# Streamed expert weights: quarters moved one seat ahead, gates stored by token tile, and transposes reordered

## What is computed

```
merged = g_pool * y_pool + g_attn * y_attn
x = x + merged @ w_out[l]
h2 = rmsnorm(x, ffn_norm_g[l])
...
for e in range(N_EXPERTS):
    g = jnp.minimum(t @ w_gate[e] + b_gate[e], SWIGLU_LIMIT)
    u = jnp.clip(t @ w_up[e] + b_up[e], -SWIGLU_LIMIT, SWIGLU_LIMIT)
    act = (u + 1.0) * (g * jax.nn.sigmoid(SWIGLU_ALPHA * g))
    out = out + comb[:, e:e + 1] * (act @ w_down[e] + b_down[e])
```

## Time and profile before

| | |
|---|---|
| median of three runs | 1081.67 us |
| profiled execution | 1081.04 us |
| its span in the trace | 1079.2 us |
| TensorE busy | 1040.2 us (96%) |
| DVE, ACT, POOL busy | 274.8, 198.6, 29.5 us |
| read from HBM | 432.14 MB |
| granted TensorE clock | 0.999 of full speed |

### The profile page before, as it was taken

How to read it: one execution, slowest core, us unless ns; L and a number is a source line. 1 busy time by engine, 2 the same in 40 slices (tenths; PEclk the granted TensorE clock), 3 DMA queues, 4 the chain that set the end, 5 groups by cost and what they waited for, 6 DMA issues and landing times.

```text
span 1079.2 us, 12157 instructions
## 1 busy us (share of the span) xinstructions
PE 1040.2 (96%) x5114; PEld 445.0 (41%) x5114; DVE 274.8 (25%) x560; ACT 198.6 (18%) x347; POOL 29.5 (3%) x41
## 2 busy tenths in 40 slices
PE   9999999999999999999999999999999999999997
PEld 5889984333333333333333333333333333333332
DVE  6876753111111111111111111111111111111121
ACT  4657532111110111111111111111111001110111
POOL 0070020000000000000000000000000000000000
PEclk9999999999999999999999999999999999999999
DMA  9835999999999999999999999999999999999996
GB/s 316 302 104 179 387 390 383 394 428 427 434 431 428 438 428 431 427 437 432 430 430 431 436 430 432 428 437 431 431 430 432 435 430 432 422 428 429 427 425 275
DMA packets 37235, 433.75 MB, mean 402 GB/s; under 512 B 5030, under 2 KB 7627, under 8 KB 19659
## 3 DMA queue, kind: packets, MB, share of 16 engines
q1 hardware_dynamic: 36704, 432.64, 95.7%
q10 hardware_dynamic: 490, 0.56, 0.1%
HBM read 432.14 MB, written 1.05 MB: 401 GB/s over the span
## 4 chain that ended last, share of the span: by engine, by line
PE 76%; DMA 12%; ACT 6%; DVE 4%; issue 1%; SPq 0%; DVEq 0%
PE ps L1027 55%; DMA ring<-in_exp_w_up 11%; PE ps L932 5%; PE ps L979 5%; ACT arena L1336 3%; PE ps L679 2%; PE ps L681 2%; PE ps L680 2%; PE ps L1035 2%; DVE ring_r L1522 2%; PE ps L973 1%; DMA ring<-in_w_in 1%; ACT ring_r L1198 1%; ACT arena L1371 1%; PE ps L941 0%
## 5 line engine op out<-in xcount | busy, mean ns | idle before, releaser
L1027 PE MATMUL ps<-ring,arena 128*64 128x512 f32 x2432 | 538.4, 595 | 15.0 <-ACT arena L1371 11.3
L1027 PEld LDWEIGHTS ps<-ring,arena 128*64 128x64 f32 x2432 | 168.0, 137 | 339.0 <-issue 316.3
L1027 PE MATMUL ps<-arena 128*64 128x512 f32 x640 | 142.0, 595 | 5.0 <-ACT arena L1371 3.1
L1773 DVE TENSOR_TENSOR arena<-ps,gain 128x512 f32<-128x512 f32 x32 | 22.1, 692 | 275.6 <-PE ps L973 275.6
L1798 DVE TENSOR_SCALAR arena<-ps 128x512 f32<-128x512 f32 x30 | 20.8, 692 | 261.8 <-PE ps L1027 261.8
L1027 PEld LDWEIGHTS ps<-arena 128*64 128x64 f32 x640 | 44.4, 137 | 89.1 <-issue 85.2
L1336 ACT COPY arena<-ps 128x512 f32<-128x512 f32 x32 | 33.8, 1055 | 249.7 <-PE ps L932 249.7
L1375 ACT COPY arena<-ps 128x256 f32<-128x256 f32 x30 | 11.2, 372 | 293.3 <-PE ps L979 293.3
L1811 DVE TENSOR_SCALAR arena<-ps 128x512 f32<-128x512 f32 x31 | 21.4, 692 | 170.9 <-PE ps L1027 170.9
L979 PE MATMUL ps<-arena 64*128 64x512 f32 x256 | 63.9, 616 | 0.0
L932 PE MATMUL ps<-arena 128*64 128x512 f32 x256 | 60.6, 593 | 0.0
(11 more groups left out here) (231 smaller groups left out, 658.7 us busy)
## 6 DMA issues: line engine op xcount, KB each, us to landing
ring<-in_exp_w_up SPq DMA_DIRECT2D x19, 4096.0 KB, 29.3
ring<-in_exp_w_down SPq DMA_DIRECT2D x18, 4096.0 KB, 28.4
ring<-in_exp_w_gate SPq DMA_DIRECT2D x18, 4096.0 KB, 29.8
ring<-in_exp_w_down SPq DMA_DIRECT2D x12, 2048.0 KB, 39.1
ring<-in_exp_w_up SPq DMA_DIRECT2D x11, 2048.0 KB, 40.4
ring<-in_exp_w_gate SPq DMA_DIRECT2D x10, 2048.0 KB, 40.7
arena<-in_exp_w_gate SPq DMA_DIRECT2D x5, 4096.0 KB, 29.8
arena<-in_exp_w_down SPq DMA_DIRECT2D x5, 4096.0 KB, 30.4
```

What stands on the lines that cost most here:

```text
L1027: last = mm(ps[BLOCK * to:BLOCK * (to + 1), bank, :], src[:, c, half, :], moved, start=(fresh and half == 0 and c == 0), stop=(half == 1 a ...
L1773: v.tensor_tensor(h_in, ps[:, 6, :].rearrange("p (c h s) -> p c h s", c=4, h=2), wide(gain[:].rearrange("p h c -> p c h"), [P, 4, 2, BLOCK ...
```

## The change

It does five things.

1. **Gates by token tile.** The 16 gate blocks, the merged rows and their high and low parts are stored tile by tile (`tile_pair`, `both_tiles`, `m_split`), through access patterns of 2 x 128 columns instead of 256. No instruction is added.
2. **Early rows.** After part (0,1) of the output projection, tile 0's halves of `early_place` and `late_place` are free. SP sends 0.5 MB to each there, and the other 0.5 MB to each after the last part.
3. **Matrices moved up by a quarter.** For n = 6 to 14 the first quarter of matrix n goes to a free seat of the hold before it (`moved_up`). Before, seat 1 of hold 0 stayed empty from the end of the first half of matrix 0 until matrix 10. For n = 11 to 14 the first quarter is sent after the first half of matrix n-5, and 3 MB after the second.
4. **The rolled loop waits one half later.** Matrix 14 has its first quarter in hold 3, and so on, so matrix 15 must wait until matrix 11 has let go of its quarter in hold 0. The rule is in the loop's code and thus holds for n = 15 to 74: each is issued after the first half of matrix n-4, no longer at the end of matrix n-5.
5. **Halves only for the last pair** (`FINE = E - 2`): the nine matrices of experts 27 to 29 come as 4 MB. And **transposes in another order** (`turns`): gather, `turn_weights`, `turn(7)`, `turn(6)`, down product.

```diff
-        FINE = E - 5
+        FINE = E - 2
@@
         def halved(n, rolled=False):
-            return not rolled and (HOLDS <= n < PASS or n >= MATRICES * FINE)
+            return not rolled and (HOLDS <= n <= 2 * HOLDS or n >= MATRICES * FINE)
+
+        def moved_up(n, q):
+            if (n, q) == (HOLDS, 0):
+                return early_place
+            if n % HOLDS == 0 and q:
+                k, p = 0, (0, 1, 3)[q - 1]
+            elif q:
+                k, p = n % HOLDS, q - 1
+            else:
+                k, p = (n - 1) % HOLDS, 2 if n % HOLDS == 1 else 3
+            return hold(k)[:, p // 2, 2 * D * (p % 2):2 * D * (p % 2 + 1)]
@@ load_matrix
-                if n >= HOLDS or not isinstance(base, int):
+                if not isinstance(base, int):
+                    sp.wait_ge(piece_done, of_round + both_halves + 1)
+                elif n >= HOLDS:
                     sp.wait_ge(piece_done, of_round + (first_half if halves else both_halves))
@@ load_first_holds
+                sp.wait_ge(wo_done, wo_count(0, 1))
+                sp.dma_start(late_place[:, 0:D], flat_rows(0)[:, 6 * D:7 * D]).then_inc(early_rows_in, 16)
+                sp.dma_start(early_place[:, 0:D], first_down[:, 0, 0:D]).then_inc(early_rows_in, 16)
@@
+                sp.wait_ge(piece_done, 2 * HOLDS)
+                sp.dma_start(moved_up(2 * HOLDS, 0), quarter_of(2 * HOLDS, 0)).then_inc(wrapped_in, 16)
+                sp.wait_ge(piece_done, 2 * HOLDS + 2)
+                sp.dma_start(hold_front[:, 0:4 * D], flat_rows(2 * HOLDS)[:, 2 * D:6 * D]).then_inc(matrix_in[0], 16)
+                sp.dma_start(moved_up(2 * HOLDS, 3), quarter_of(2 * HOLDS, 3)).then_inc(lower_in[0], 16)
+                for n in range(2 * HOLDS + 1, PASS):
+                    k = n % HOLDS
+                    sp.wait_ge(piece_done, 2 * (n - HOLDS) + 1)
+                    sp.dma_start(moved_up(n, 0), quarter_of(n, 0)).then_inc(quarter_in[k][0], 16)
+                    sp.wait_ge(piece_done, 2 * (n - HOLDS) + 2)
+                    sp.dma_start(hold(k).rearrange("p h x -> p (h x)")[:, 0:6 * D],
+                                 flat_rows(n)[:, 2 * D:]).then_inc(matrix_in[k], 16)
@@ tensor
+            def turns(i):
+                pe.wait_ge(pick_ready, i + 2)
+                gather()
+                pe.wait_ge(expert_step, 2 * i + 2)
+                turn_weights(5)
+                pe.wait_ge(act_ready, i + 1)
+                turn(7, act_out).then_inc(act_T, 1)
+                pe.wait_ge(hg_ready, i + 2)
+                turn(6, h_got).then_inc(h_turned, 1)
@@ expert
-                pe.wait_ge(pick_ready, i + 2)
-                gather()
-                pe.wait_ge(act_ready, i + 1)
-                turn(7, act_out).then_inc(act_T, 1)
-                turn_weights(5)
+                turns(i)
                 pe.wait_ge(actT_ready, i + 1)
                 product(r, step, MATRICES * j + 2, 7, actT, fresh=True)
-                pe.wait_ge(hg_ready, i + 2)
-                turn(6, h_got).then_inc(h_turned, 1)
```

More of the change, by code:

```diff
@@ L173, in build, with tile_pair, both_tiles @@
         y_split = pair(places["u"], places["p"], NG)
-        m_split = pair(places["gate"], places["gate"] + NC * S, NC)
+        tiles = gate.rearrange("p c s -> p (c s)").rearrange("p (b t c s) -> p b t c s", b=2, t=NT, c=NC)
+        m_split = tuple(rounded(places["gate"] + NC * S * b, NC * S).rearrange("p (t c s) -> p t c s", t=NT, c=NC)
+                        for b in range(2))
+        def tile_pair(m):
+            return tiles[:, m // NC, :, m % NC, :]
+        def both_tiles(ap):
+            return ap.rearrange("p (t s) -> p t s", t=NT)
         h_normed = gate[:, 0:NC, :]
@@ L889, in project @@
                         columns_of = both(split_slot(WO_P), ALL, m)
-                    last = mm3(wo_sum(t, half, part), both(m_split, ALL, m, slice(P * t, P * (t + 1))), columns_of,
+                    last = mm3(wo_sum(t, half, part), both(m_split, ALL, t, m), columns_of,
                                start=(m == 0), stop=(m == NC - 1))
@@ L993, in product @@
                 first_pass = isinstance(r, int) and isinstance(step, int)
+                moved_on = first_pass and HOLDS <= n < 3 * HOLDS
                 by_quarters = first_pass and HOLDS <= n < 2 * HOLDS
@@ L1003, in product @@
                                     pe.wait_ge(landed, r * 16 + 16)
-                        if by_quarters and c == 0:
-                            pe.wait_ge(quarter_in[at][half], 16)
+                        if c == 0 and (by_quarters or moved_on and half == 0):
+                            pe.wait_ge(*((wrapped_in, 16) if n == 2 * HOLDS else (quarter_in[at][half], 16 * (n // HOLDS))))
                         if n == HOLDS - 1 and first_pass and half == 0 and c == 0:
@@ L1008, in product @@
                         if n == 0 and first_pass and half == 1 and c == 2:
+                            pe.wait_ge(early_rows_in, 32)
                             pe.wait_ge(last_quarter_in, 16)
-                        if n not in TAIL and c == (2 if by_quarters else 0):
+                        if n not in TAIL and c == (2 if moved_on else 0):
                             if half == 0:
@@ L1019, in product @@
                             row = late_place[:, D * (c - 2):D * (c - 1)]
-                        elif n == HOLDS and first_pass and half == 0:
-                            row = early_place[:, D * c:D * (c + 1)] if c < 2 else hold_chunks(at)[:, 0, c - 2, :]
+                        elif moved_on:
+                            row = moved_up(n, 2 * half + c // 2)[:, D * (c % 2):D * (c % 2 + 1)]
                         for to in range(2):
@@ L1247, in gate_tanh @@
                 strip_wait(act, s)
-                strip_release(fn(gate[:, c, :], strip_bank(s)[:, 0:S], ACT.Tanh, bias=hgate[:, c:c + 1], scale=0.5), s)
+                strip_release(fn(tile_pair(c), both_tiles(strip_bank(s)[:, 0:S]), ACT.Tanh, bias=hgate[:, c:c + 1], scale=0.5), s)
             def group_hi():
@@ L1316, in _ @@
                 act.wait_ge(merged, m + 1)
-                nc.scalar.copy(m_split[0][:, m, :], gate[:, NC + m, :]).then_inc(m_hi, 1)
+                nc.scalar.copy(m_split[0][:, :, m, :], tile_pair(NC + m)).then_inc(m_hi, 1)
             def squares2(t, half, part=0):
```

50 lines of the change are left out of this document (29 added, 21 removed).

## The result

The changed kernel takes 1086.96 us (median of five runs, 1086.11 to 1087.35) where the kernel before took 1081.67 (five runs, 1081.14 to 1082.17): 1.0045 times as long, with a 95% interval of 1.0034 to 1.0057. That is 5.3 us slower, 0.8 us more than forecast and inside the range. The profiled execution took 1086.7 us, 5.7 more than the one before.

The account below looks back on a forecast made before the run. Bound: the weight stream's delivery of up 29, then TensorE's path. Stream lag +3.6, whole up 29 +1.6, transposes -0.6 give +4.6 us on the profiled 1081.04; the median adds 0.6: 1086.2 us, 8-in-10 range 1083.2 to 1088.5.

Parts of the forecast that it names:

- The mechanism: At matrix 15: later issue finds the queue empty or nearly so; the stream's lag stays until up 29 starts at its landing.
- The stream's lag, the first term: At matrices 15 and 16: the later wait makes the stream 3.6 us late, between 2.3 and 4.7.
- The three rows taken as nearest: Matrices 1 to 3, 4 MB each: 12.9, 14.1 and 15.2 us to land; 14.1 taken for matrix 15's empty queue.
- the rival of more than one gap: Matrix 17 or 18 also finds the queue empty, adding another 2 to 3 us: 1089 us; chance 5%.
- Rival 2: At matrix 15: the empty queue costs little, landing after 11.7 us, matrix 16 1.1 us late: 1083.7 us; chance 12%.
- Rival 3: After matrix 15: matrix 17 or 18 finds the queue empty too, 2 to 3 us more: 1089 us; chance 5%.
- The transposes: In each expert: reordering saves 0.56 us, bounds 0.3 and 0.75; at the end it counts once, behind up 29.
- Halves only for the last pair: At expert 29: up 29 comes as one transfer, and TensorE starts only at its landing: +1.6 us.
- the two terms +3.6 and +1.6: At the end: stream lag and up 29's whole landing simply added, the stream's last pieces taken to stay ahead of TensorE.
- Early rows and gates by tile: In the front: early rows' gain, at most 2.4 us, ends at matrix 15; gates cost nothing, -0.5 to +0.5 us.
- The moved quarters: From about 181 us: the stream runs 2.4 us ahead while limited by releases; the gain ends at matrix 15.

Follow-up runs that it names:

- The first variant: Kernel before, with only the rolled loop's transfers (n = 15 to 74) waiting one half of a matrix longer; 1088.61 us, ratio 1.0059.
- The second: Kernel after, with only matrices 15 to 19 keeping the late wait, 20 to 74 waiting as before; 1087.08 us, ratio 1.0047.
- the lead kept: Kernel after, matrices 15 to 18 sending three quarters at matrix n-5's end, one half a matrix later; halves from expert 27: 1080.09 us; whole transfers: 1081.98.
- the lead was kept with the old transposes: Kernel after, matrices 15 to 18 sending only one quarter late, halves from expert 27, transposes ordered as in the kernel before; 1082.56 us, ratio 1.0003.

## Why the prediction was right, and where it was off

**The mechanism held.** Matrix 15 was issued at 279.98 (forecast 278.9, "278 to 280") into an empty queue, the traffic dipped at 275 to 285, latencies grew from 14.4 us on, and up 29 started at 1004.73 (forecast 1003 to 1005) at its landing. The waits for up matrices rose to 18.4 us (forecast 15 to 25). The first of them came at 595 us; before, it came at 795, so 200 us sooner and not 100. The first variant shows the cause by itself: the late wait, alone, costs 6.5 us. The second shows that the same wait costs nothing from matrix 20 on.

**The stream's lag, the first term: 3.6 us forecast, 4.4 at matrix 16 and 4.6 at matrix 17 measured.** It is inside the bounds (2.3 to 4.7), but three parts of its working were off and partly cancelled:

- Matrix 15 left 1.1 us later than forecast. Expert 0's up product began 0.34 us later (183.56 instead of 183.22), three experts became 0.45 us shorter and not 0.56, and the down product follows ACT's copy 0.12 us later. The last 0.3 us lie between the end of the half product and the issue, a step that the prediction put at nothing; before, it took 0.2 us (273.72 to 273.92).
- It then took 12.4 us, not 14.1. Four executions with matrix 15 issued just behind or into the end of matrix 14 gave 12.3 to 12.6. The three rows taken as nearest all had other transfers in front of them; the shortest, 12.9, was the right one to take, with the others as bounds. The fit of the Trainium skill ("DMA: Bandwidth & Descriptors", "Anatomy of one DMA"), an estimate of 11.6 us, was 0.8 us short of this and nearer than 14.1. The Trainium skill gives this fit for transfers issued by GpSimd; these are issued by SyncE.
- Matrix 16 was taken to land one transfer (9.7 us) after matrix 15. It landed 11.2 us after it. An issue 3.2 us before the landing of the one in front is still too late for a seamless queue. The prediction put 302.4 us as what its own issue allows, and so did see that this was near; it should have priced a second, shallow hole, as it did in the rival of more than one gap.

**Rival 2 was half right.** The empty queue cost matrix 15 little, as it said (12.4 us; the rival had 11.7). It fell by matrix 16: the queue has to be empty but once, but its refilling costs twice. **Rival 3** named the wrong matrix: matrix 17 had enough in hand, as calculated; what was short was matrix 16.

**The transposes: 0.56 us per expert forecast, 0.45 measured.** Between the gathers of experts 0 to 3 the chain has 27.35 us instead of 27.80. The timeline of the kernel after in expert 0, beside the earlier trace rows: start us, us, engine, line, and in brackets the idle time ahead.

```profile
192.41 1.05 ACT L1382 COPY arena<-ps 128x512 f32<-128x512 f32 x1 [7.80 <-PE ps L979]
...
193.51 0.66 PE L1020 MATMUL ps<-con,arena 128*128 128x128 f32 x4 [0.20 <-ACT arena L1382]
194.10 7.09 PE L1076 MATMUL ps<-ring,arena 128*64 128x512 f32 x32
201.12 1.99 PE L1026 MATMUL ps<-arena 64*128 64x512 f32 x8
```

The down product starts 1.69 us after ACT's copy starts, where it was 1.57 us; the forecast had both equal. The rest is as forecast: the scatter follows the down product without the 0.58 us of transposes between them.

**Halves only for the last pair: +1.6 us forecast.** In the kernel before it costs 1.5 us, with the lead kept 1.9, both near the price. In the changed kernel itself it costs only 0.8, as far as overlapping intervals can tell. There the last pieces of the stream are ahead of TensorE, as the prediction says, but by little: up 31's first piece landed at 1058.9, and its product starts at 1060.38. Without the whole transfers TensorE comes sooner and waits for it. So the two terms +3.6 and +1.6 do not simply add. That step of the sum failed, by some 0.8 us too much; the lag was 1.0 us too small. That the total came out only 0.8 us short is in part luck.

**Early rows and gates by tile** cost and brought nothing, as forecast. **The moved quarters** did bring their lead, some 2 us at 230.7 us, but it ended at matrix 10, in a hole that the prediction did not see, and not at matrix 15. Since matrix 15's landing is set by its own issue, this changed nothing in the time. Nor did the prediction have a term for what the runs with the lead kept show, that the gain needs the shorter experts.

**Where the 5.3 us are.** Whole transfers and the rest without moved quarters: +1.5 (the variant without them, 1083.73 against 1082.26). Moved quarters with the late wait: +3.3 (1086.96 against 1083.73, across chips). This leaves 0.5 us, no more than the medians of the kernel before differ between the chips (1081.67 to 1082.26).

## What to carry to other kernels

Where a queue of transfers is fed by buffers that come free, look for the last moment at which it runs empty or nearly so, and price an edit by what has landed by then; afterwards a deeper queue brings nothing, and what was lost there is paid at the end. A rule written for the one boundary at which it is needed (here, a seat still taken by the matrix before) should split off just the piece that it concerns: one quarter sent late cost nothing that could be measured, a whole matrix sent late 6.5 us. Two terms at the end of a program, the transfer that lands late and the engine that starts late, are a maximum and not a sum, so each edit there has to be priced with the other in place.

## What the runs showed of the hardware

**How early the next transfer must be issued.** Matrix 16's issue, 3.2 and 2.6 us before the landing in front of it, gave steps of 11.2 and 11.0 us instead of 9.7. In the kernel after, the middle 2 MB of matrix 10, issued 2.2 us before the piece in front landed, had a step of 7.2 us where 2 MB take 4.9. Not every such issue costs: matrix 3, issued 3.0 us before the landing in front in the kernel after, had a step of 9.8, and in the kernel before, issued 3.1 us before it, one of 12.1. The kernel after's matrix 17, issued 7.0 us before the landing in front, had a step of 9.8. Where the lead was kept with the old transposes, the last quarter of matrix 16 was issued 4.7 us before the landing in front of it and cost 0.3 us. In these traces the cost is gone at about 5 us.

**The rate does not depend on depth.** Apart from single delayed ones (below), transfers of 4 MB land 9.71 to 9.72 us apart, at latencies of 17 as of 42 us. Cut into two, 4 MB take 9.8 us.

**Single transfers are delayed.** Every execution has one to three transfers that take 0.6 to 1.6 us longer than the rest. The places differ, but not freely: the two traces of the kernel before have the same transfer delayed (landed at 455.6 and 455.9, steps of 10.8 and 10.5 us), and so have two of the variants (landed at 446.6 and 445.8, steps of 11.3 and 10.4). In the kernel after it is the one issued at 923.28 (DMA issues at 914.89 and 923.28 us):

```profile
ring<-in_exp_w_down SPq DMA_DIRECT2D x1, 4096.0 KB, 40.1
...
ring<-in_exp_w_gate SPq DMA_DIRECT2D x1, 4096.0 KB, 42.5
```

They land at 955.0 and 965.8, a step of 10.8 us. In the kernel before it was the one landed at 455.6 (10.8), in the first variant those at 345.4 (11.0) and 993.3 (2 MB in 6.0). While the stream decides, each of them should go to the end in full. This fits the scatter of 1 to 3 us between executions of one kernel; what delays them stays open.

**TensorE's clock after a wait.** With the transposes in the new order, TensorE's idle time gathers in one wait of 1.7 us per expert once the stream decides (1.3 us in the old order, where the rest is idle in front of other instructions). After some of these waits the granted clock falls. The kernel after, one such product in the timeline, and a window over its middle:

```profile
857.86 8.79 PE L1076 MATMUL ps<-ring,arena 128*64 128x512 f32 x32 [1.72 <-DMA ring<-in_exp_w_up]
```

```profile
858.00:862.00 4.00, 4.00 (x12) 1.16 (x12) 0.01 (x1) 0.00 (x0) 0.00 (x0) 0.58 1.01 434
```

The up product takes 8.79 us instead of 7.09. Over 858 to 862 us the granted clock is 0.58, which is mostly the lower of the two levels, 1.2 GHz; at the end of the product it is back at 2.4 GHz (0.99 over 862 to 867). It happened three times in the kernel after and four times in that with the transposes alone, and never after the 1.3 us waits of the first variant. Here it costs nothing, since the engine waits for the stream again before the end. In the variant of the kernel after with halves from expert 27 on, the last such product started at 888.16 and took 8.78 us, and TensorE's path from there runs without a wait for a transfer to up 29 at 1002.75: up 29 came 1.7 us later by it, and the wait for up 31 hid this.
